# Smaller pieces for the weight sums, and another split of the last step's work, in a two-block layer kernel

## What is computed

```python
for i in range(2):
    h = x * (1 + scale) + shift                    # from the modulation
    y = mla_mixer(h, ...) if i == 0 else s5_mixer(h, ...)
    x = layer_norm_2(ALPHA * x + (1 + gate) * y, ln_mix_g[i], ln_mix_b[i])
    h = x * (1 + scale_f) + shift_f
    a = relu(h @ w1[i] + b1[i])                    # 512 tokens, 1024 -> 4096
    y = (a * a) @ w2[i] + b2[i]                    # 4096 -> 1024
    x = layer_norm_2(ALPHA * x + (1 + gate_f) * y, ln_ffn_g[i], ln_ffn_b[i])
```

## Time and profile before

| | us |
|---|---|
| median of 3 runs | 2663.14 (2659.13 to 2665.58) |
| the profiled execution, its own time | 2667.46 |
| its span from the first to the last instruction | 2665.7 |
| TensorE busy | 2477.4 (93% of the span) |
| VectorE busy | 1819.8 (68%) |
| ScalarE busy | 1161.3 (44%) |
| GpSimd busy | 73.7 (3%) |

### The profile page before, as it was taken

One profiled execution on the slowest core, in us unless ns is written; L12 is line 12 of the kernel. 1 busy time (PEld: TensorE's weight loads), 2 busy tenths in 40 slices (PEclk: granted clock), 3 DMA queues, 4 the chain that ended last, 5 costly groups with the idle time before them and its releaser, 6 DMA issues. The chain is left out here.

```text
span 2665.7 us, 33669 instructions
## 1 busy us (share of the span) xinstructions
PE 2477.4 (93%) x13175; PEld 1967.5 (74%) x13175; DVE 1819.8 (68%) x2585; ACT 1161.3 (44%) x1626; POOL 73.7 (3%) x174
## 2 busy tenths in 40 slices
PE   7999999999999999899988799999999889999996
PEld 5666678777777877788875357788888877787884
DVE  4899545588875666899955465677765674665568
ACT  5444422255564234688853243622324144444432
POOL 0000000000000001000001000000000000000000
PEclk9999999999999988899999899999999889999998
DMA  7887627233326724999962943794331504243443
GB/s 262 269 283 272 236 84 281 82 111 88 90 93 210 260 37 189 356 414 414 415 238 84 262 94 99 180 251 143 118 103 59 160 18 143 80 143 109 127 158 118
DMA packets 305967, 475.15 MB, mean 178 GB/s; under 512 B 29035, under 2 KB 194398, under 8 KB 295825
## 3 DMA queue, kind: packets, MB, share of 16 engines
q1 hardware_dynamic: 285392, 409.29, 45.1%
q0 software_dynamic: 15888, 54.53, 7.2%
q10 hardware_dynamic: 4528, 9.18, 0.9%
HBM read 431.82 MB, written 74.69 MB: 190 GB/s over the span
## 5 line engine op out<-in xcount | busy, mean ns | idle before, releaser
L2380 DVE TENSOR_TENSOR expert_parts<-w,expert_parts 128x2048 fp32r<-128x2048 f32 x102 | 232.7, 2288 | 24.2 <-ACT expert_parts L2376 23.4
L1345 PE MATMUL banks<-h_parts,ssm_parts 128*128 128x512 f32 x960 | 228.9, 395 | 0.8 <-DVE ssm_parts L1612 0.4
L3782 PE MATMUL banks<-big,late_parts 128*128 128x512 f32 x960 | 221.1, 392 | 2.2 <-DVE late_parts L3935 2.2
L2376 ACT ACTIVATE expert_parts<-w 128x2048 fp32r<-128x2048 f32 x102 | 194.7, 1915 | 63.9 <-PE banks L2387 53.8
L3782 PEld LDWEIGHTS banks<-big,late_parts 128*128 128x128 f32 x960 | 181.2, 189 | 41.2 <-DVE late_parts L3935 2.4
L1345 PEld LDWEIGHTS banks<-h_parts,ssm_parts 128*128 128x128 f32 x960 | 178.4, 188 | 43.3 <-issue 6.5
L2387 PE MATMUL banks<-expert_parts,expert_xt 128*128 128x512 f32 x816 | 193.4, 397 | 4.2 <-DVE expert_xt L2368 4.2
L2387 PEld LDWEIGHTS banks<-expert_parts,expert_xt 128*128 128x128 f32 x816 | 154.3, 191 | 37.0 <-DVE expert_xt L2368 4.8
L3782 PE MATMUL banks<-h_parts_second,late_parts 128*128 128x512 f32 x720 | 164.9, 389 | 2.4 <-DVE h_parts_second L3959 2.4
L4181 PE MATMUL banks<-h_parts_second,late_parts 128*128 128x512 f32 x512 | 159.4, 393 | 4.1 <-DVE h_parts_second L4395 2.4
L3782 PEld LDWEIGHTS banks<-h_parts_second,late_parts 128*128 128x128 f32 x720 | 135.1, 188 | 30.5 <-issue 2.5
(11 more groups left out here) (792 smaller groups left out, 4741.3 us busy)
## 6 DMA issues: line engine op xcount, KB each, us to landing
w_second<-in_mlp_w_dram SPq DMA_DIRECT2D x60, 1024.0 KB, 5.3
w<-in_w_exp_gate_dram SPq DMA_DIRECT2D x34, 1024.0 KB, 8.6
w<-in_w_exp_up_dram SPq DMA_DIRECT2D x34, 1024.0 KB, 8.2
w<-in_w_exp_down_dram SPq DMA_DIRECT2D x34, 1024.0 KB, 8.3
w<-in_w_in_dram SPq DMA_DIRECT2D x64, 512.0 KB, 4.6
w<-in_mod_mix_w_dram SPq DMA_DIRECT2D x24, 1024.0 KB, 5.2
w<-in_mod_ffn_w_dram SPq DMA_DIRECT2D x23, 1024.0 KB, 6.0
w<-in_w_in_dram SPq DMA_DIRECT2D x16, 1024.0 KB, 5.6
```

The source lines that it names most:

```text
L1345: mm = pe.matmul(ps[:, t % 2, :], parts[:, t % SPLITS, w, kk, :], k.hp[:, x, kk, :], start=(kk == 0 and j == 0), stop=(kk == KD - 1 and j ...
L2376: act.activation(self.high_part(h), self.raw(h), ACT.Copy).then_inc(self.high_done, 1)
L2380: dve.tensor_tensor(self.low_part(h), self.raw(h), self.high_part(h).bitcast(F32), ALU.subtract).then_inc(self.low_done, 1)
L3782: mm = pe.matmul(ps[:, bank(n, f), :], w_part(n, w)[:, kk, f * P:(f + 1) * P], x[:, v, kk, :], start=(first_chunk(n) and kk == 0 and j == ...
```

## The change

The sums: nothing is formed in the attention any more. All four are formed behind the first tail's norm, in pieces of 1 MB, step by step of the scheme: for each of the four steps `two`, `right`, `three` and `four`, a copy and an addition each, 32 transfers, and GpSimd waits for each one before it issues the next.

The squares of the hidden layer become two ScalarE operations behind the two relus, and `combine` keeps its four sums. A square waits until `hidden_low` of the pair before has read the tile that it writes.

The turns of x go four at a time behind the up pieces 16 and 17 instead of two at a time behind 16 to 19.

In the last step the residual of half 0 of each row tile (products 11 and RIGHT) is added by DMAs from GpSimd that accumulate onto the row tile (`x_late` for row tiles 2 and 3, `x_early` for 0 and 1, 256 KB each); half 1 stays on VectorE. The statistics of row tiles 0 and 1 move to ScalarE: a pass over 128x1024 for the negated mean and one for the squares, with accumulators. All four row tiles' `last_norm` come behind the last product. A join of two sums on VectorE moves one piece ahead. Semaphore names and new small tiles are left out of the diff.

```diff
@@ -3282,10 +3282,6 @@
                     first_half(k, sp, i // 2, ahead)
-
-        @block.gpsimd
-        def _(pool):
-            sums.form_first(pool)
@@ -3623,33 +3617,22 @@
-    def form_first(self, pool):
-
-        s = self.sem
-        view = lambda t: t.rearrange("(s p) n -> s p n", p=P)
-        two, right = view(self.two), view(self.right)
-        pool.dma_start(two, self.block(0, 0)).then_inc(s["sum_two"], 16)
-        pool.dma_start(right, self.block(0, 1)).then_inc(s["sum_right"], 16)
-        pool.wait_ge(s["sum_two"], 16)
-        pool.dma_start(two, self.block(0, 1), accum_op=ALU.add).then_inc(s["sum_two"], 16)
-        pool.wait_ge(s["sum_right"], 16)
-        pool.dma_start(right, self.block(1, 1), accum_op=ALU.add).then_inc(s["sum_right"], 16)
-        pool.wait_ge(s["sum_two"], 32)
-        pool.wait_ge(s["sum_right"], 32)
-
-    def form_rest(self, pool):
-
-        s = self.sem
-        view = lambda t: t.rearrange("(s p) n -> s p n", p=P)
-        two, three, four = (view(t) for t in (self.two, self.three, self.four))
-        pool.dma_start(three, two).then_inc(s["sum_three"], 16)
-        pool.wait_ge(s["sum_three"], 16)
-        pool.dma_start(three, self.block(1, 1), accum_op=ALU.add).then_inc(s["sum_three"], 16)
-        pool.wait_ge(s["sum_three"], 32)
-        pool.dma_start(four, three).then_inc(s["sum_four"], 16)
-        pool.wait_ge(s["sum_four"], 16)
-        pool.dma_start(four, self.block(1, 0), accum_op=ALU.add).then_inc(s["sum_four"], 16)
-        pool.wait_ge(s["sum_four"], 32)
+    def form(self, pool):
+
+        n = 0
+        for i in range(K2 // KD):
+            tiles = slice(i * KD // 2, (i + 1) * KD // 2)
+            two, three, right, four = (t.rearrange("(s p) n -> s p n", p=P)[tiles] for t in (self.two, self.three, self.right, self.four))
+            for dst, src in ((two, self.block(0, 0)[tiles]), (right, self.block(0, 1)[tiles]), (three, None), (four, None)):
+                if src is None:
+                    src = two if dst is three else three
+                pool.dma_start(dst, src).then_inc(self.formed, 16)
+                n += 1
+                pool.wait_ge(self.formed, 16 * n)
+                last = self.block(*((0, 1) if dst is two else (1, 0) if dst is four else (1, 1)))[tiles]
+                pool.dma_start(dst, last, accum_op=ALU.add).then_inc(self.formed, 16)
+                n += 1
+                pool.wait_ge(self.formed, 16 * n)
@@ -3773,7 +3756,7 @@
             pool.wait_ge(s["x_low"], KD)
-            later.form_rest(pool)
+            later.form(pool)
@@ -4174,6 +4157,14 @@
             step(pool.tensor_tensor(vec[:, X_SHIFT], vec[:, X_SHIFT], vec[:, ROOM], ALU.add))
+            pool.wait_ge(s["x_copied"], 2 * TB)
+            for first, done, ready in ((2, "x_late", 2), (0, "x_early", 4)):
+                pool.wait_ge(s["scaled"], ready)
+                for t in (first, first + 1):
+                    pool.dma_start(z(t, 0).rearrange("p (c n) -> p c n", n=P), x_tile(t, 0), accum_op=ALU.add).then_inc(s[done], 16)
+            for done in ("x_late", "x_early"):
+                pool.wait_ge(s[done], 32)
+
         @block.tensor
@@ -4267,12 +4258,12 @@
                     g = UP * up(n)[0] + up(n)[1] - UP - 1
-                    if 0 <= g < TB:
+                    if 0 <= g < 2:
                         if g == 0:
                             pe.wait_ge(s["z_step"], PER_STEP)
-                        turn(2 * g)
-                        turn(2 * g + 1)
+                        for t in range(4 * g, 4 * g + 4):
+                            turn(t)
                 elif n == N - DOWN:
@@ -4303,12 +4294,15 @@
                 g = UP * i + m
-                if g:
-                    act.wait_ge(s["squared"], g)
                 for f in range(HT):
                     act.activation(r[:, f, :], ps[:, bank(n, f), :], ACT.Relu, bias=k.cols[:, at:at + 1]).then_inc(s["relu_done"], 1)
+                if g:
+                    act.wait_ge(s["hidden_low"], g)
+                for f in range(HT):
+                    act.wait_ge(s["relu_done"], HT * g + f + 1)
+                    act.activation(q[:, f, :], r[:, f, :], ACT.Square).then_inc(s["squared"], 1)
@@ -4354,30 +4348,41 @@
                     g = UP * i + m - UP - 1
-                    if 0 <= g < TB:
-                        copy_turned(2 * g)
-                        copy_turned(2 * g + 1)
+                    if 0 <= g < 2:
+                        for t in range(4 * g, 4 * g + 4):
+                            copy_turned(t)
                 else:
-            def root_of(t):
-                act.wait_ge(s["mean_ready"], t + 1)
-                act.activation(root[:, t:t + 1], agg[:, t, 1:2], ACT.Ln, bias=k.eps_ln[:]).then_inc(s["log_done"], 1)
+            def root_of(t, variance, scale):
+                if t < 2:
+                    act.wait_ge(s["var_ready"], t + 1)
+                else:
+                    act.wait_ge(s["mean_ready"], t - 1)
+                act.activation(root[:, t:t + 1], variance, ACT.Ln, scale=scale, bias=k.eps_ln[:]).then_inc(s["log_done"], 1)
                 act.wait_ge(s["log_done"], t + 1)
-            for t in range(TB):
-                root_of(t)
+            act.wait_ge(s["x_early"], 32)
+            act.wait_ge(s["early_summed"], 2)
+            room = e[:, 0:4].rearrange("p v t -> p (v t)")
+            for t in range(2):
+                act.activation(room, z_row(t), ACT.Copy, scale=-1.0 / D, accum_out=nmean[:, t:t + 1]).then_inc(s["mean_done"], 1)
+                act.wait_ge(s["mean_done"], t + 1)
+                act.activation(room, z_row(t), ACT.Square, bias=nmean[:, t:t + 1], accum_out=var[:, t:t + 1]).then_inc(s["var_ready"], 1)
+                root_of(t, var[:, t:t + 1], 1.0 / D)
+            for t in range(2, TB):
+                root_of(t, agg[:, t, 1:2], 1.0)
             sums_step = Steps(dve, s["z_step"])
-            joined = Steps(dve, s["joined"])
+            joined, scale_step, early = (Steps(dve, s[x]) for x in ("joined", "scaled", "early_summed"))
             end = Steps(dve, s["last_step"])
@@ -4395,12 +4400,7 @@
             def combine(g):
-                dve.wait_ge(s["relu_done"], HT * (g + 1))
-                if g:
-                    dve.wait_ge(s["hidden_low"], g)
-                flat = e[:, 0:4].rearrange("p (c h) t -> p c (h t)", c=2)
-                dve.tensor_tensor(flat, r[:], r[:], ALU.mult).then_inc(s["squared"], 1)
-                dve.wait_ge(s["squared"], g + 1)
+                dve.wait_ge(s["squared"], HT * (g + 1))
                 n = comb.start(dve.tensor_tensor(e[:, LEFT], e[:, FIRST], e[:, SECOND], ALU.subtract))
@@ -4435,16 +4435,18 @@
-            def gated(q):
-
-                first, half = {PRODUCT_11: (2, 0), PRODUCT_22: (2, 1), PRODUCT_RIGHT: (0, 0), PRODUCT_TWO: (0, 1)}[q]
+            def scaled(q):
+
+                half = {PRODUCT_11: 0, PRODUCT_22: 1, PRODUCT_RIGHT: 0, PRODUCT_TWO: 1}[q]
                 for j in range(2):
-                    joined.start(dve.tensor_tensor(total(q, j), total(q, j), gate_of(half), ALU.mult))
+                    scale_step.start(dve.tensor_tensor(total(q, j), total(q, j), gate_of(half), ALU.mult))
+
+            def with_residual(q, done):
+                first = {PRODUCT_22: 2, PRODUCT_TWO: 0}[q]
                 for j in range(2):
-                    joined.after(joined.n - (1 if j == 0 else 0))
+                    scale_step.after(scale_step.n - 1 + j)
                     row = total(q, j).rearrange("p (c n) -> p c n", n=P)
-                    end.start(dve.tensor_tensor(row, row, x_tile(first + j, half), ALU.add))
-                end.after(end.n)
+                    done.start(dve.tensor_tensor(row, row, x_tile(first + j, 1), ALU.add))
@@ -4472,29 +4474,25 @@
                         dve.wait_ge(s["gate_loaded"], 16)
-                        dve.wait_ge(s["x_copied"], 2 * TB)
-                        gated(PRODUCT_11)
+                        scaled(PRODUCT_11)
                 elif p == PRODUCT_FOUR:
                     take(PRODUCT_RIGHT, n)
-                    gated(PRODUCT_RIGHT)
-                    for t in range(2):
-                        statistics(t, 0)
+                    scaled(PRODUCT_RIGHT)
                 elif p == PRODUCT_TWO:
+                    dve.wait_ge(s["x_copied"], 2 * TB)
                     take(PRODUCT_TWO, n)
+                    scaled(PRODUCT_TWO)
+                    with_residual(PRODUCT_TWO, early)
                     take(PRODUCT_22, n)
-                    gated(PRODUCT_TWO)
-                    for t in range(2):
-                        statistics(t, 1)
-                    for t in range(2):
-                        mean(t)
                 elif p == PRODUCT_22:
                     take(PRODUCT_22, n)
-                    gated(PRODUCT_22)
+                    scaled(PRODUCT_22)
+                    with_residual(PRODUCT_22, end)
+                    end.after(end.n)
```

(28 more changed lines are left out.)

## The result

The change made the kernel slower: **2902.25 us** median of 4 runs (2900.31 to 2915.38) against 2663.81 us of the kernel before (2659.13 to 2665.58). The ratio is 1.091, 95% interval 1.0891 to 1.0929. Predicted were 2652.9 us, 2643 to 2661.

A forecast was written before the change was run, and what follows sets the result against it. TensorE, busy for 93% of the span, was taken as the bound. The terms -12.7 + 0 - 1.8 + 9.6 - 5.3 = -10.2 us, from the median of 2663.14, gave 2652.9 us, range 2643 to 2661.

The forecast's parts named there:

- part 2: Tail stage: 32 transfers of 1 MB, priced by size at 194 to 322 us, fit the 373.7 us free; 0 us.
- rival (a): Tail stage: the chain of 32 transfers outlasts the tail, slower from 12.2 us a piece, 2695 us at 13; chance 0.06.
- The weight loads are covered by their own lead: Tail stage: weight loads beside the sums, 17.0 us each beside 4 MB pieces, make TensorE wait 0 us.
- Part 1: Latent attention: without the first two sums TensorE's wait for wkv ahead of head 2 goes; -12.7 us.
- Part 3: Closing stage's first steps: squares on ScalarE relieve VectorE, and TensorE's 1.76 us wait for the relu goes; -1.8 us.
- part 4: Closing stage: four turns in a step stall TensorE twice behind ScalarE's copies and slow its clock; +9.6 us.
- Part 5: Last step: VectorE, full to the end, sheds residual additions to GpSimd's DMAs and statistics to ScalarE; -5.3 us.
- the second pair of additions: Last step: GpSimd's second pair of DMA additions lands late, takes the gain back, about 2661 us; rival with chance 0.13.

The follow-up runs named there:

- eight: The changed kernel with its 1 MB pieces cut as 8 tiles by 64 rows instead of 4 by 128; 2679.98 us, ratio 1.0062 to the kernel before.
- large: The changed kernel with 8 transfers of 4 MB, 16 tiles outermost, in place of 32 of 1 MB; 2682.53 us, ratio 1.0065 to the kernel before.
- wide: The changed kernel with the 128 rows outermost instead of the 4 tiles in all 32 transfers; 2652.97 us, ratio 0.9958 to the kernel before.
- b_squares: The kernel before with only the squares of the hidden layer moved to ScalarE; one run of 2663.13 us.
- wide_early: `wide` with ScalarE's copies of turned tiles right behind the relus instead of at the step's end; 2638.22 us, ratio 0.9896 to the kernel before.

## Why the prediction was wrong

**The step that failed is part 2's price,** "I take it by size, since all these bytes go through the same engines", with its 194 to 322 us. The chain lasted 623 us: the bytes went through a quarter of the engines. A 4 MB transfer with 16 tiles outermost was scaled down to one with 4, and no row of before shows a transfer of that shape. The text had the other end in hand, 774 us at the full 4 MB times, and let an argument, not a row, take it out of the range. With 373.7 us free between those ends the outcome was open, and 0.06 for rival (a) was far too little. Its rule was right: 12.4 us a piece is slower by 0.6% (`eight`), and at 19.5 us it gives 2653 + 32 x (19.5 - 11.7) = 2903; measured are 2902. With the rows outermost the step's own range holds: 278 us, so its allowance of up to 4 us a transfer for start and landing came to (278 - 194) / 32 = 2.6 us, the loads beside included. The estimate of 4.4 us a transfer (141 us in all) by the Trainium skill, "DMA: Bandwidth & Descriptors", section "Anatomy of one DMA", fits none of the three shapes: it was 8.7 us a piece even with the rows outermost.

"The weight loads are covered by their own lead" failed too, and was hidden by the larger miss. The 110 us that the earlier trace rows show beside two sums are no measure of four: in the changed kernel loads took 15.1 us in the median from 1670 to 2072 us, and TensorE waited 15.3 us for weight parts in that stretch, where the kernel before has no such wait. `large` shows such waits without any narrow transfer, from 1799 on, and before the sums were through by 1783. With the rows outermost the step holds: `wide` has no such wait behind the start of the sums.

**The other parts came out near their prices.**

Part 1: TensorE's start of head 0 in the changed kernel:

```profile
1469.20 3.54 PE L3294 MATMUL banks<-cq,latent_attention_wq 128*64 128x512 f32 x4 [6.46 <-DMA latent_attention_wkv<-in_mla_w_kvb_dram]
```

Its waits in the attention (1420 to 1610 us):

```profile
PE banks L3294 <- DMA latent_attention_wkv<-in_mla_w_kvb_dram: 6.5, 1, 6.5
```

Head 0's wait is 6.46 us against 7.01, and none ahead of head 2 is left. The tail's sums start 15.4 us earlier (1670.17 against 1685.58), of which 2.3 us were there ahead of the stage (1472.04 - 7.01 against 1469.20 - 6.46): 13.1 us, predicted 12.7.

Parts 3 to 5: the chain of the closing stage, of the kernel before (two lines not shown yet) and of after (start, us):

```profile
2243.27 23.59 PE banks L4181 x96
...
2601.68 9.53 PE banks L4199 x42
```

```profile
2473.95 24.58 PE banks L4172 x96
...
2589.03 38.08 PE banks L4190 x168
2627.11 10.90 PE banks L4172 x48
...
2643.68 1.97 PE banks L4237 x8
2645.64 11.49 PE banks L4172 x48
...
2687.72 38.08 PE banks L4190 x168
...
2840.04 19.05 PE banks L4190 x84
```

Part 3: from the start to the first down block 2589.03 - 2473.95 = 115.1 us, before 2359.38 - 2243.27 = 116.1; 1.0 us less, predicted 1.8. The wait for the relu is gone, which `b_squares` showed to be worth 2.0 at that spot; here the stage's first 96 matmuls took 24.58 us instead of 23.59, and that hides the other 1.0. `b_squares` also showed why little of it is kept without part 4.

Part 4: from the first down block to the second 98.7 us, before 88.1, 10.6 more; the second one takes 38.08 instead of 39.98, 1.9 less: +8.7, predicted +9.6. TensorE's waits of the stage:

```profile
PE banks L4237 <- ACT x L4314: 9.6, 2, 4.8
```

The stretches around the two stalls (length, busy us of PE, PEld, DVE, ACT, POOL, clock, DMA share, GB/s):

```profile
2640.00:2648.00 8.00, 4.33 (x17) 3.84 (x18) 5.53 (x6) 5.30 (x6) 0.00 (x0) 0.79 0.28 107
2659.00:2667.00 8.00, 4.20 (x14) 3.71 (x15) 5.66 (x6) 5.43 (x6) 0.00 (x0) 0.58 0.32 122
```

Two waits of 4.8 us, each with a dip of the granted clock (0.79 and 0.58, part of the time at 1.2 GHz): eight transposes took 1.97 us instead of 1.03, and no wait ahead of the second block, all as written. What the prediction took as given, that the order of ScalarE's queue is the price, `wide_early` shows to be the cause.

Part 5: from the last step's first product 2898.6 - 2840.04 = 58.6 us, before 2665.7 - 2601.68 = 64.0: 5.5 less, predicted 5.3 (its terms 2.66 + 1.29 + 1.52 add to 5.5, not to the 5.4 that it wrote). Its doubt, whether the second pair of additions lands in time, is answered by GpSimd, ScalarE and VectorE in order of time:

```profile
2869.19 2.57 POOL L4164 DMA_DIRECT2D big_plain<-x  x2 [1.58 <-DVE big_plain L4442]
...
2874.86 1.06 ACT L4373 ACTIVATE closing_e<-big_plain 128x1024 f32<-128x1024 f32 x1 [8.92 <-DVE big_plain L4449]
...
2885.45 1.23 DVE L4512 SCALAR_TENSOR_TENSOR big_plain<-big_plain,closing_nmean,h_parts_second_plain 128x1024 f32<-128x1024 f32 x1
```

The DMA issues of 2860 to 2885 us (KB each, median us to landing):

```profile
big_plain<-x POOLq DMA_DIRECT2D x2, 256.0 KB, 4.2
```

They landed in 4.2 us, ScalarE's first pass waited for VectorE and not for them, and VectorE has no gap ahead of its norms.

Parts 3 to 5 together: from 2243.27 and 2473.95 to the end 422.4 and 424.7 us, +2.2, predicted +2.5. The predicted sum of -10.2 us is what `wide` does: -11.2 (-15.4 to -6.9).

## What to carry to other kernels

When a transfer is cut smaller, write down the shape that is issued: what was measured with 16 tiles outermost did not carry over to 8 or 4, and putting the 128 rows outermost, one other order in the view, took the whole loss back. Where a price is known from both sides and the free time lies between the ends, the chance of the bad side is not small, however good the argument for the near end. And before a group of operations is called dear, see what stands ahead of its releaser in the queue of the engine that serves it: moving four copies ahead of the squares, the weight copy and the high part was worth 12 us in the traces of `wide` and `wide_early`.

## What the hardware showed that I had not expected

- A lone 1 MB addition from DRAM to DRAM with 4 tiles outermost took 25.0 us, and 1552 of its 2064 packets are under 512 B; with 8 tiles outermost there were 528 small ones of 1040.
- The copies from one sum to another, same 4 tiles outermost but one unbroken run of memory on both sides, ran wide all the same. In the changed kernel one took 6.3 us alone, where a copy from the weights took 13.5; its DMA share was 0.49 (2230.8 to 2237 us, columns as in the stretches above). That the unbroken run is the reason is argued, not shown:

```profile
2230.80:2237.00 6.20, 0.00 (x0) 0.00 (x0) 0.00 (x0) 0.00 (x0) 0.52 (x1) 0.50 0.49 169
```

- The same sums beside the same loads cost TensorE 20.7 to 24.3 us of waits in 4 MB pieces, one behind the other, and nothing in 1 MB pieces with the rows outermost, though the larger ones are done 71 to 78 us sooner. Size is not all: 1 MB pieces that run narrow cost waits too, 15.3 us with 4 tiles outermost and 4.5 with 8.
